# Moving a gate-value product from GpSimd to VectorE in a hybrid decoder layer, and list scatters ahead of a power

## The reference

```python
h = modulate(rms_norm(x, g_mix), sh1, sc1)
z = h @ w_in                      # 1024 -> 1536: u, v and gt, 512 columns each
d, new_pool = multi_scale_pool(u, pool_prev, prev_valid)   # trailing means of 2, 4, 8, 16 minus u
a = v * jax.nn.sigmoid(gt)        # the gate-value product
yc, new_conv = causal_depthwise_conv(a, conv_prev, w_dw, b_dw)   # 31 taps a channel
yn = layer_norm(yc); conv_out = jax.nn.silu(yn)
x = x + g1 * (concat([pool_out, conv_out]) @ w_out)
h2 = modulate(rms_norm(x, g_ffn), sh2, sc2)
idx, wts = route(h2)              # 8 of 64 experts a token
```

## Time and profile before

| | |
|---|---|
| median of 3 runs | 3226.58 us (3219.52 to 3230.39) |
| span of the profiled execution, first to last instruction | 3224.1 us |
| time of that execution around its span | not recorded; the median lies 2.5 us above the span |
| busy share of the span: TensorE, VectorE, GpSimd, ScalarE | 83%, 55%, 36%, 33% |
| GpSimd's products (L501) | 224.2 us in 32 instructions |
| taps of one convolution (L903) | 47.59 us, 120 instructions |

### The profile page before, as it was taken

The page is one execution under the profiler, slowest core; times in us unless marked ns, Lnnn a source line. Parts: engine busy times, 40 slices in busy tenths (PEclk is TensorE's granted clock), DMA queues, the critical chain, the costliest instruction groups (busy, mean ns, idle before and its releaser), DMA issues.

```text
span 3224.1 us, 56738 instructions
## 1 busy us (share of the span) xinstructions
PE 2685.4 (83%) x11753; PEld 2015.7 (63%) x11754; DVE 1778.0 (55%) x3601; ACT 1058.2 (33%) x2213; POOL 1147.3 (36%) x1173
## 2 busy tenths in 40 slices
PE   6897787778777839999999998989999999999940
PEld 1174564555565517877777777777777777777730
DVE  1034785785677754355554466565645544445558
ACT  1022212112111213244443355454534443344411
POOL 0025525644753342323233322223332232232337
PEclk9998898898887769999999999999999999999975
DMA  7751001001000306567776688888887677667665
GB/s 267 294 228 43 30 33 53 20 33 59 7 33 33 121 16 191 116 193 226 220 214 181 187 253 245 230 254 241 252 225 217 194 211 207 182 177 195 174 177 203
DMA packets 255795, 518.50 MB, mean 161 GB/s; under 512 B 18222, under 2 KB 154375, under 8 KB 255588
## 3 DMA queue, kind: packets, MB, share of 16 engines
q1 hardware_dynamic: 199108, 327.34, 29.4%
q0 software_dynamic: 56624, 190.48, 24.7%
HBM read 386.48 MB, written 131.99 MB: 161 GB/s over the span
## 4 chain that ended last, share of the span: by engine, by line
PE 53%; POOL 15%; DMA 12%; issue 10%; DVE 5%; ACT 3%; ACTq 1%; DVEq 1%; POOLq 1%; SPq 0%
PE zb L1465 22%; PE mx L1465 11%; PE zb L1299 7%; POOL b_av L501 7%; DMA b_xg<-hf_d,b_gidx 5%; PE tp L1478 4%; POOL list_d L511 4%; DMA acc_d<-b_ob,b_sidx 3%; PE mx L1321 3%; PE zb L1263 2%; DMA b_big<-in_w_ada 2%; PE zb L1414 1%; ACT b_wh L794 1%; DVE b_wl L1168 1%; POOL b_pa L484 1%
## 5 line engine op out<-in xcount | busy, mean ns | idle before, releaser
L595 POOL DMA_INDIRECT acc_d<-b_ob,b_sidx x180 | 310.8, 1727 | 1067.2 <-DVE b_ob L1193 556.4
L1465 PE MATMUL zb<-b_wh,b_xh 128*128 x1448 | 589.7, 407 | 53.3 <-issue 33.8
L1465 PE MATMUL zb<-b_wh,b_xl 128*128 x1448 | 572.8, 396 | 0.0
L1465 PE MATMUL zb<-b_wl,b_xh 128*128 x1448 | 572.2, 395 | 0.0
L1168 DVE TENSOR_TENSOR b_wl<-b_win,b_wh (+1 forms) x780 | 481.3, 687 | 132.1 <-ACT b_wh L794 131.8
L794 ACT CAST b_wh<-b_win (+1 forms) x780 | 419.8, 621 | 147.0 <-issue 113.3
L1299 PE MATMUL zb<-b_hT,b_win 128*128 128x256 f32 x1536 | 364.9, 402 | 95.6 <-ACT b_sgt L671 94.6
L1299 PEld LDWEIGHTS zb<-b_hT,b_win 128*128 128x128 f32 x1536 | 310.7, 204 | 149.0 <-ACT b_sgt L671 97.4
L903 DVE SCALAR_TENSOR_TENSOR b_y<-b_a_buf,b_wdw,b_y 128x256 f32<-128x256 f32 x960 | 380.7, 481 | 0.0
L1465 PEld LDWEIGHTS zb<-b_wh,b_xh 128*128 128x128 f32 x1448 | 273.5, 189 | 131.3 <-issue 72.6
L1145 DVE SCALAR_TENSOR_TENSOR b_hh<-b_sgx,b_lt,zb 128x256 f32<-128x256 f32 x181 | 86.9, 480 | 477.7 <-ACT b_sgx L779 476.5
(11 more groups left out here) (242 smaller groups left out, 3211.8 us busy)
## 6 DMA issues: line engine op xcount, KB each, us to landing
b_win<-in_w_gate SPq DMA_DIRECT2D x64, 1024.0 KB, 6.3
b_win<-in_w_up SPq DMA_DIRECT2D x64, 1024.0 KB, 12.4
b_win<-in_w_down SPq DMA_DIRECT2D x64, 1024.0 KB, 14.5
b_big<-in_w_ada SPq DMA_DIRECT2D x12, 2048.0 KB, 9.0
acc_d<-b_x1b SPq DMA_DIRECT2D x1, 9216.0 KB, 35.0
b_xin<-in_x_prompt SPq DMA_DIRECT2D x16, 512.0 KB, 3.2
b_big<-in_w_ada_final SPq DMA_DIRECT2D x4, 2048.0 KB, 8.1
b_xres<-in_x_prompt SPq DMA_DIRECT2D x16, 512.0 KB
```

Of the source, the lines that this page charges most:

```text
L595: G.indirect_dma_start(acc_d, bass.IndirectOffsetOnAxis(ap=sidx[1 - j][:, 0:1], axis=0), ob[1 - j][:], None, compute_op=ALU.add).then_inc( ...
L1465: last = M.matmul(o, lhs, rhs, start=(first and n == 0), stop=(final and n == len(terms) - 1))
```

## The change

The product moves from GpSimd to VectorE, where it takes the place of the copy into `a_buf`: `conv` multiplies `sgt` by `vv` straight into it, and waits for ScalarE's drains instead of `a_ready`. `sgt` and `vv` get four buffers instead of two, `av` goes. ScalarE waits once in a step, before the first sigmoid, until the convolution of the group before has taken its product (`a_taken`). On GpSimd the four differences stand one behind the other, then the scatters, then the LN powers, then the x1 powers.

```diff
-    av = f("av", [P, CH, SUP]); a_buf = f("a_buf", [P, CH, CONVB + SUP]); u_buf = f("u_buf", [P, CH, POOLB + SUP])
+    a_buf = f("a_buf", [P, CH, CONVB + SUP]); u_buf = f("u_buf", [P, CH, POOLB + SUP])
...
-    sgt = f("sgt", [P, 2, SUP]); vv = f("vv", [P, 2, SUP]); pa = f("pa", [P, 2, POOLB + SUP])
+    sgt = f("sgt", [P, CH, SUP]); vv = f("vv", [P, CH, SUP]); pa = f("pa", [P, 2, POOLB + SUP])
...
-        def amul(s, j, post):
-
-            zv = z.now + (CH if post else 0) + CH + 2 * j + 1
-            pool.wait_ge(S["z_drained"], zv + 1)
-            if post:
-                pool.wait_ge(S["a_taken"], s)
-            G.tensor_tensor(av[:, j, :], sgt[:, j % 2, :], vv[:, j % 2, :], ALU.mult).then_inc(S["a_ready"], 1)
...
             if has_in:
-                for j in range(CH):
-                    amul(s, j, has_post)
-                    if j < CH - 1:
-                        diff(s, j, first, has_post)
+                for g_ in range(CH):
+                    diff(s, g_, first, has_post)
+            z.step((CH if has_post else 0) + (ZC if has_in else 0) + (TPS if has_post else 0))
+            if has_scatter:
+                scatter(s - 3)
             if has_post:
                 for j in range(TPS):
                     power(st[:, 6:7], st[:, 7:8], S["lnv"], lt_i.now + j + 1, S["lnr"])
-            if has_in:
-                diff(s, CH - 1, first, has_post)
-            z.step((CH if has_post else 0) + (ZC if has_in else 0) + (TPS if has_post else 0))
-            if has_scatter:
-                scatter(s - 3)
...
-                if not (first and j < 2):
-                    act.wait_ge(S["a_ready"], CH * s + j - 1)
-                A.activation(sgt[:, j % 2, :], zb[z.n % 2][:, 0:SUP], ACT.Sigmoid).then_inc(S["z_drained"], 1)
+                if j == 0 and not first:
+                    act.wait_ge(S["a_taken"], s)
+                A.activation(sgt[:, j, :], zb[z.n % 2][:, 0:SUP], ACT.Sigmoid).then_inc(S["z_drained"], 1)
...
-                A.copy(vv[:, j % 2, :], zb[z.n % 2][:, 0:SUP]).then_inc(S["z_drained"], 1)
+                A.copy(vv[:, j, :], zb[z.n % 2][:, 0:SUP]).then_inc(S["z_drained"], 1)
...
-            dve.wait_ge(S["a_ready"], CH * p + CH)
+            dve.wait_ge(S["z_drained"], ZC if first else (CH + ZC + TPS) * p + ZC - TPS)
             if not first:
                 chain(V.tensor_copy(a_buf[:, :, 0:CONVB], a_buf[:, :, SUP:SUP + CONVB]))
-            V.tensor_copy(a_buf[:, :, CONVB:CONVB + SUP], av[:]).then_inc(S["a_taken"], 1)
+            V.tensor_tensor(a_buf[:, :, CONVB:CONVB + SUP], sgt[:], vv[:], ALU.mult).then_inc(S["a_taken"], 1)
```

More of the change, by code:

```diff
@@ L146, in program @@
         mix_filled mix_drained lg_filled lg_drained rk_filled rk_drained xsq xms xrs xn_ready lnv lnr
-        x1_ready x1_sq x1_ms x1_rs h2_ready a_ready a_taken d_ready conv_link m_ready pairs_ready
+        x1_ready x1_sq x1_ms x1_rs h2_ready a_taken d_ready conv_link m_ready pairs_ready
         pool_const dve_const sm_x sm_h sm_state sm_y edge_tp edge_ready
```

## The result

The changed kernel takes 3292.93 us (median of four runs, 3281.53 to 3313.89), the kernel before in the same comparison 3225.13 us (3219.52 to 3230.39): a ratio of 1.0221, interval 1.0183 to 1.0259. The profiled execution took 3281.53 us; its span is 3279.6 us, 55.5 us over the 3224.1 of before. The comparison by steps is made between these two spans.

A forecast was written before the change was run, and what follows sets the result against it. GpSimd's gate-value multiply, held to the end of VectorE's taps, was taken to bound the kernel. Steps 3 to 7 +101, 1 and 2 +3, 8 +0.5: +104.5 us on the 3224.1 us span, median 3331 us, range 3304 to 3358.

The forecast's parts named there:

- I take it to be held until the taps end: GpSimd's first pooling difference (L484), arriving under VectorE's convolution taps, waits for their end; likeliest case, chance 0.86.
- +20.2: Net us added in each of steps 3 to 7: LN power 24.7 us later, 4.5 us coming back behind it.
- Step 8: Scatters without differences start before and under the taps: +0.5 us if hidden, +18.8 us as upper bound if all held.
- a scatter seems to pass between two instructions: GpSimd scatters under VectorE's taps: at most half a microsecond each, so sixteen fit under 47.59 us.
- 37.64 forecast: Us of held add, differences and sixteen scatter issues on GpSimd between the taps' end and the first LN power.
- 39.73: Us from first LN power to ScalarE's square of the second tile, taken from step 8 of before for all steps.
- the wait of 11.79 us: VectorE's wait after the taps for the transposed convolution output; forecast to clear as TensorE's input projection runs through.
- Steps 1 and 2: Steps with differences but no scatter: LN power +3.4 us, shorter way behind it, net +1.4 us each, +3 together.
- The microsecond a step: Allowance at the upper end of the range, an estimate, if TensorE is slower after standing longer.
- The turns: Rival, chance 0.05: GpSimd operations and VectorE taps alternate, each tap waiting; 3245 us at most, 3190 if half blocks.
- the case that it gave 0.02: Something between held and passing: an add or two slipping in at the head of the taps; chance 0.02.
- 3226.6 - 97 + 114: Median before, less 97 us if differences and scatters pass under taps (chance 0.07), plus 114 us of lengthened convolutions.

## Why the prediction was off

**The step that failed** is "I take it to be held until the taps end", taken for the first difference of all seven steps on the strength of seven held multiplies. Those came 17 us and more into the taps. The difference comes when ScalarE has copied its input, and the trace of before showed that this falls at the head of the taps, between 0.3 us ahead of the first one and 3.3 us behind it in steps 1 to 7:

```profile
221.11 0.37 ACT L665 COPY b_u_buf<-zb 128x256 f32<-128x256 f32 x1 [3.88 <-PE zb L1299]
...
561.34 0.37 ACT L665 COPY b_u_buf<-zb 128x256 f32<-128x256 f32 x1 [5.08 <-PE zb L1299]
```

In step 1 the copy ends 3.27 us after the first tap, in step 4 0.64 us after it. In step 4 of the changed kernel it ends 1.30 us ahead of the first tap (578.77 against 580.07):

```profile
578.40 0.37 ACT L653 COPY b_u_buf<-zb 128x256 f32<-128x256 f32 x1 [5.16 <-PE zb L1287]
```

Of that turn of 1.9 us, 1.05 are taps that start later after the square of the step before (12.38 us against 11.33; the product has 0.53 of it), and 0.89 are a copy that ends earlier after it (11.08 against 11.97), since TensorE begins the projection 0.61 us earlier; why it does is open. A microsecond either way decides. I argued about what happens to an operation that comes late, and never asked when this one comes. Four steps at +5.3 to +7.1 instead of +20.2 are 56.8 us less.

**Step 8** failed by the other term: "a scatter seems to pass between two instructions", and sixteen to fit under the taps. Under the 120 taps of step 8 one passed and the next stood 46.02 us. The step cost +11.8 us, inside its bounds of 0.5 and 18.8, because five were out before the hold. The Trainium skill ("SBUF — State Buffer", "Who interferes with whom") infers that a `tensor_tensor` doesn't stop descriptor generation. That can't be carried over to the scatters under these taps, which read two SBUF tensors as well: they stood 33.74 and 46.02 us, to 0.83 us behind the last tap. A scatter also takes its row numbers from `rows` in SBUF, and whether that reading or the descriptors had to wait isn't shown.

**What held.** Where the add was held (step 3), the LN power came 36.85 us behind the taps (37.64 forecast) and the step cost +18.4 (20.2). The way from LN power to square is 39.5 to 40.1 us in steps 3 to 7 (39.73). VectorE's product took 1.23 us, TensorE's input projection ended at 620.1, 13.5 us before the end of step 4's taps, and the wait of 11.79 us became 1.21 us. Steps 1 and 2 were -0.4 us together (+3). The microsecond a step that the range allows for a slower TensorE isn't seen: the way to the square stays within 0.4 us of its forecast.

**The sum.** Against +104.5: steps 4 to 7 -56.8, step 3 -1.8, steps 1 and 2 -3.4, step 8 +11.3, behind it +1.8: +55.6, the 55.5 of the spans but for rounding.

**The turns.** Steps 4 to 7 took the turns that the prediction gave 0.05, and they began as in the case that it gave 0.02, with an add slipping in at the head of the taps. As a rival the turns were priced at the differences' full 16.3 us per step as an upper end (3226.6 - 97 + 114 is 3244 us, and 3187 with half of it, close to the 3245 and 3190 given); steps 4 to 7 paid 5.95 us of longer taps for four differences and two scatters, about a third. The Trainium skill's rule (same section) that issue order decides agrees with the runs that made the add late and early. Its other half, that the one behind waits for one whole instruction, doesn't: the held add of step 3 waited for some 115 taps. A break between two taps lets a late operation in, but it isn't the only way: the differences of steps 4 to 7 followed the first add in between taps that overlap. By these runs the forecast for a step should have been a choice between +18 to +21 (late) and +5 to +7 (early), by arrival.

**Why slower at all.** The LN power is what the step waits for, and the change queues sixteen scatter issues of 20.2 us ahead of it. The hold decides how much of that is left behind the taps: nothing with a break in them, thirteen scatters in steps 4 to 7, all sixteen and the differences in step 3. Either a break in the taps (3192 us) or the LN powers first (3132 us) takes that away; the second also leaves the taps undisturbed, 47.6 instead of 55 us in seven steps. With step 8's 1.8 us that is a sum of about 55 us of taps, beside 60 us between the two medians; that the one accounts for the other is argued, not shown.

## What to carry to other kernels

When an operation is moved off a busy engine, ask of the next one in its queue when it arrives, to the microsecond, and not only whether it can be delayed. Put what the critical path waits for (here the LN power) ahead of work that only has to be done sometime, and place that work under stretches without a long row of VectorE instructions that read two SBUF tensors each. Where it can't move, a break every few instructions in a long row of VectorE's two-operand instructions lets GpSimd in, at 4 to 8% of the row (in step 8, 1.8 us of 47.6 for the short one-operand instructions, 3.6 for the waits).

## What the runs showed of the hardware

- Overlapping two-operand instructions of VectorE (one each 0.396 us, 0.08 to 0.10 us before the end of the last) held a GpSimd add or product that came after the head of their row to its end: up to 47.34 us. With a break of 0.036 us after every fourth, no operation took over 2.1 us.
- Indirect-DMA issues on GpSimd can be held in the same way: 33.74 us in step 4, 46.02 us in step 8.
- In the rows without breaks, an add that came up to 0.28 us after the first two-operand tap passed, and one at 0.75 us or later was held. Why 0.28 us is still early enough isn't shown.
- Once one add had passed, what followed it on GpSimd within 0.21 us passed too, between overlapping taps: twenty operations in step 4, none over 1.03 us. What lets them in without a break stays open, and so does why some scatters pass (two in step 4 after the differences, one in step 8 at 0.9 us) and the next doesn't.
